# Gate matmuls between the up-phase tiles: groups of four quads at 24 tiles, in place of one or two quads at each of 77

## The reference, cut to what matters

```
s1, i1 = top_k(s[:, :, 0], 16);  s2, i2 = top_k(s[:, :, 1], 16)   # per head, 128 keys each
top, pos = top_k(s1 + s2 over 16x16, 16)                          # 8 heads x 16 = 128 routes a token
eidx  = (i1 * 128 + i2) at pos;  gates = softmax(top)
act   = gelu(x . u[eidx])
out   = sum over routes of (gates * act) * v[eidx]
```

## Time and profile before

| | |
|---|---|
| median of 3 runs | 3015.55 us (3014.22, 3015.55, 3023.57) |
| span of the profiled execution | 3015.1 us |
| TensorE matmul busy | 2968.4 us (98%) |
| VectorE busy | 2369.0 us (79%) |
| ScalarE busy | 1201.5 us (40%) |
| GpSimd busy | 1315.3 us (44%) |
| gate matmuls (L1702) | 1536, from 517.6 to 882.7 us in layer 0 and from 2068.8 to 2433.9 us in layer 1 |

### The profile page before, as it was taken

How to read it: one execution, slowest core, us unless ns; L and a number is a source line. 1 busy time by engine, 2 the same in 40 slices (tenths; PEclk the granted TensorE clock), 3 DMA queues, 4 the chain that set the end, 5 groups by cost and what they waited for, 6 DMA issues and landing times.

```text
span 3015.1 us, 43969 instructions
## 1 busy us (share of the span) xinstructions
PE 2968.4 (98%) x16132; PEld 2622.5 (87%) x16132; DVE 2369.0 (79%) x4437; ACT 1201.5 (40%) x1878; POOL 1315.3 (44%) x749
## 2 busy tenths in 40 slices
PE   8999999999999999999999999999999999999999
PEld 6668999999998888888888888999999997888887
DVE  7436899988886888888356737999888968888887
ACT  5434333444443333333435643334444433333333
POOL 4213465444434444443346533564434434544441
PEclk9999999999999999999999999999999999999999
DMA  4203367999999999999321122558999999999996
GB/s 147 69 29 105 105 203 263 341 370 361 375 368 368 381 362 354 366 356 338 105 98 43 35 84 85 172 175 319 364 371 362 375 360 374 363 354 377 360 362 223
DMA packets 345861, 800.83 MB, mean 266 GB/s; under 512 B 27952, under 2 KB 192048, under 8 KB 345392
## 3 DMA queue, kind: packets, MB, share of 16 engines
q1 hardware_dynamic: 271776, 529.49, 50.0%
q0 software_dynamic: 73728, 268.47, 23.6%
q10 hardware_dynamic: 144, 0.07, 0.0%
HBM read 695.15 MB, written 102.76 MB: 265 GB/s over the span
## 4 chain that ended last, share of the span: by engine, by line
PE 91%; DVE 3%; DMA 3%; ACT 1%; issue 1%; SPq 0%; POOL 0%; DVEq 0%; ACTq 0%
PE PS L1522 28%; PE PS L1524 27%; PE PS L1523 27%; PE PS L1702 3%; DMA arena<-acts_dram 1%; DMA gates_dram<-arena 1%; PE PS L1773 1%; PE PS L1679 1%; PE PS L1656 1%; DVE resid L1031 1%; PE PS L1639 1%; PE PS L1638 0%; ACT arena L654 0%; PE PS L1646 0%; POOL w_lo L567 0%
## 5 line engine op out<-in xcount | busy, mean ns | idle before, releaser
L1522 PE MATMUL PS<-x_hi,w_hi 128*128 128x384 f32 (+1 forms) x2616 | 927.0, 354 | 8.7 <-POOL w_lo L567 4.0
L1524 PE MATMUL PS<-x_hi,w_lo 128*128 128x384 f32 (+1 forms) x2616 | 907.4, 347 | 0.0
L641 ACT ACTIVATE w_hi<-w_raw 128x1024 fp32r<-128x1024 f32 x609 | 643.0, 1057 | 661.0 <-PE PS L1524 645.2
L1523 PE MATMUL PS<-x_lo,w_hi 128*128 128x384 f32 (+1 forms) x2616 | 905.6, 346 | 0.0
L578 POOL DMA_INDIRECT arena<-in_v_t,arena x256 | 443.0, 1731 | 566.4 <-DVE resid L1294 515.2
L1522 PE MATMUL PS<-w_hi,x_hi 128*128 128x512 f32 x1744 | 679.5, 390 | 7.6 <-DVE x_lo L1311 7.5
L1524 PE MATMUL PS<-w_hi,x_lo 128*128 128x512 f32 x1744 | 678.6, 389 | 0.0
L1523 PE MATMUL PS<-w_lo,x_hi 128*128 128x512 f32 x1744 | 678.5, 389 | 0.0
L567 POOL TENSOR_TENSOR w_lo<-w_raw,w_hi 128x1024 fp32r<-128x1024 f32 x169 | 420.5, 2492 | 549.4 <-ACT w_hi L641 549.3
L1271 DVE TENSOR_TENSOR w_lo<-w_raw,w_hi 128x1024 fp32r<-128x1024 f32 x440 | 536.9, 1220 | 110.5 <-ACT w_hi L641 110.3
L578 POOL DMA_INDIRECT arena<-in_u_rows,arena x256 | 382.6, 1495 | 485.6 <-DVE arena L1278 432.3
(11 more groups left out here) (186 smaller groups left out, 2358.2 us busy)
## 6 DMA issues: line engine op xcount, KB each, us to landing
w_raw<-in_u_t SPq DMA_DIRECT2D x256, 512.0 KB, 7.0
w_raw<-in_v_t SPq DMA_DIRECT2D x256, 512.0 KB, 5.7
acts_dram<-arena SPq DMA_DIRECT2D x256, 192.0 KB, 7.4
gates_dram<-arena SPq DMA_DIRECT2D x24, 2048.0 KB, 16.3
arena<-gates_dram SPq DMA_DIRECT2D x64, 768.0 KB, 7.7
arena<-acts_dram SPq DMA_DIRECT2D x256, 192.0 KB, 7.3
w_raw<-in_hg_t SPq DMA_DIRECT2D x40, 512.0 KB, 3.2
w_raw<-in_pq_t SPq DMA_DIRECT2D x32, 512.0 KB, 3.3
```

Source lines behind the costliest of these rows:

```text
L641: act.activation(w_hi[:, slot, :], w_raw[:, slot, :], ACT.Copy).then_inc(hi_ready, 1)
L1522: pe.matmul(ps, wh, xh, start=start, stop=False)
L1523: pe.matmul(ps, wh, xl, start=False, stop=False)
L1524: return pe.matmul(ps, wl, xh, start=False, stop=stop)
```

## The change

`quads_before` now rises in steps of four. A whole group of four quads (32 matmuls) is issued ahead of 24 of the tiles 44, 47, 50, 53, 57, ... 117 (19 distances of three tiles, four of four), in place of one quad at 58 and two quads at 19 of the 77 tiles from 41 to 117. ScalarE's moves and SyncE's stores go by the same function. The two octets of a group are built at VectorE's steps one and two after the group before it (`octets_at`), and at steps 41 and 42 for the first. The matmuls, their operands, the number of moves, stores and octets are the same.

```diff
+def steps_before(tile, count, first, end):
+    return count * min(max(tile - first, 0), end - first) // (end - first)
+
 def quads_before(tile):
-    return QUADS * min(max(tile - FIRST_QUAD, 0), END_QUAD - FIRST_QUAD) // (END_QUAD - FIRST_QUAD)
+    return 4 * steps_before(tile, QUADS // 4, FIRST_QUAD, END_QUAD)
+
+def group_at(group):
+    return next(tile for tile in range(NKEYS) if quads_before(tile + 1) > 4 * group)
+
+def octets_at(step):
+    first = [FIRST_QUAD] + [group_at(g) + 1 for g in range(QUADS // 4 - 1)]
+    return [2 * g + b for g, at in enumerate(first) for b in range(2) if step == at + b]
...
-                octet = 0
                 for s in range(FIRST_DVE_LOW - RING + 1, 2 * NKEYS):
...
-                    while octet < QUADS // 2 and 2 * octet < quads_before(s + 2):
+                    for octet in octets_at(s):
                         make_onehots(octet)
-                        octet += 1
```

## The result

In executions of both kernels on the same chip the changed kernel took 3025.51 us (median of 16 runs, 3018.05 to 3034.16), the kernel before 3018.0 us (median of 16, 3013.5 to 3023.86). The ratio is 1.0027, interval 1.0019 to 1.0035. Forecast were 3007.1 us and a range up to 3011.5. The forecast stood on 3015.55 us, the median of three runs of the kernel before; its sixteen give 3018.0, so 2.5 us of the distance between 3007.1 and 3025.51 are the starting point's.

What follows compares the result with a forecast made beforehand. TensorE, busy 98% of the span, was taken as the bound. Removing 106 visits at 0.080 us saves 8.5 us, all else nothing: 3015.1 - 8.5 = 3006.6, with the median 0.5 above, 3007.1 us; range 3004.8 to 3011.5.

Steps and rivals of the forecast that it cites:

- The unit costs: TensorE's gate matmuls: fixed 0.080 us per visit, 0.447 per quad, 1.87 per group; 106 visits removed save 8.5 us.
- Rival 3: TensorE's gate matmuls: a run of 32 goes slower past its 16th matmul; net +24 us, 3039 us; chance 0.04.
- Rival 4: TensorE's gate runs: the further matmuls gain 1.9 us by dense running, 3005.2 us; chance 0.03.
- ScalarE's moves cost nothing: ScalarE: four moves in a row end at V + 4.0 (V: group start), before Gelu is due at V + 6.0; no cost.
- VectorE's octets cost nothing: VectorE: same number of octets, moved by up to two steps, hidden behind three tiles of up matmuls; no cost.
- SyncE's queue: ... Not moved, no new wait: SyncE: gate stores are issued at multiples of eight quads, on the same tiles in both orders; no cost.
- It does not fall behind for good: VectorE: its work over three tiles with a group sums to 13.1 of 14.35 us, so it keeps up.
- The octets' slack: VectorE: a group's second octet ends 2.9 us before the next group is due; today's has 3.9 us.
- Rival 1: Ahead of gate matmuls TensorE waits for an octet delayed through Gelu's late stores; 4 us given back, 3011 us; chance 0.08.
- Rival 2: Start of the value phase: last gate store and loads behind it fixed in time, gain all lost, 3015.5 us; chance 0.05.

Runs made afterwards that it cites:

- experiment 11: The changed kernel with each gate store one SyncE step (one tile) earlier, still 2 MB on SyncE's queue: 3000.55 us, ratio 0.9946 to the kernel before.
- experiment 3: The changed kernel with ScalarE's four moves behind the Gelu and `w_hi` of their step instead of ahead: 3023.98 us, ratio 1.0022 to the kernel before.
- experiment 6: The changed kernel without the low f16 part of the second one-hot in VectorE's octets, TensorE reading the high part twice: 3027.19 us, ratio 1.0032.
- experiment 4: The changed kernel with groups of two quads, each with one octet, made two steps ahead as before: 3017.6 us, ratio 0.9996 to the kernel before.
- experiment 7: The changed kernel with only the last gate store of each layer on ScalarE's queue: 3025.92 us, ratio 1.0032 to the kernel before.
- experiment 1: The changed kernel with all gate stores issued from ScalarE's queue instead of SyncE's: 3005.8 us, ratio 0.9953 to the kernel before.
- experiment 5: The changed kernel with each gate store cut into four 512 KB parts on SyncE's queue: 3006.65 us, ratio 0.9963 to the kernel before.
- experiments 1 and 2: Gate stores on ScalarE's queue, in the changed kernel (3005.8 us, ratio 0.9953) and in the kernel before (3013.45 us, 0.9988).

## Why the prediction was wrong

- **The unit costs (0.080 us per visit, 0.447 per quad, 1.87 per group): right.** 1.86 us for 45 of 48 groups, and in experiment 11 the 8.46 us arrive whole.
- **Rival 3, a run past its 16th matmul goes slower: refuted.** 32 in a row go at the pace of 8. The figure of 81 ns that the Trainium skill gives ("TensorE: Matmul & The Clock Gate", section "Back-to-back issue gap") doesn't hold in these runs either: the trace shows 55.3 to 55.8 ns. Rival 4, denser running, didn't come either.
- **ScalarE's moves cost nothing: right,** by experiment 3. VectorE's octets cost nothing by their load, as far as experiment 6 can show it; by their place they do, as the next two points say.
- **"SyncE's queue: ... Not moved, no new wait": this is the step that failed.** The tile of the gate store is unchanged, as I wrote. But a step of SyncE waits for a `w_lo`, and the gate store now goes out between two `w_lo` with no octet between them, behind the group's second octet: 3.2 us later against TensorE's tiles, and 1.6 us ahead of the next load, not 4.2. Gelu's room fell from 7.7 to 4.8 us by it. I counted the position in the order and not the time. Nor did I look at what stands behind the gate store: its 21.06 us in the chain and Gelu's longest wait for a store, 4.5 us, were both read, and not connected. The timeline of SyncE in the kernel before shows the hold (593.59, 4.83 us) and would have priced it.
- **"It does not fall behind for good": wrong for the loop.** VectorE's own sum, 13.1 of 14.35 us, is right, but the loop of store, Gelu, `w_hi`, `w_lo` and SyncE has no such slack. The octets' slack was worked out as 2.9 us from one undisturbed place; by the starts in the trace its least is 0.1 us where TensorE doesn't wait, and 2.7 before (behind the first two octets of a layer). In experiment 11, where the loop is left in peace, it is 3.6 us and more at all but one of them (1.8).
- **Rival 1 was the right mechanism with the wrong size.** I took Gelu's five late stores as fixed in number and in length (1.8 us), and counted coincidences. They aren't fixed: the change makes them 22, up to 8.9 us. Three groups wait, which is fewer than the five a layer that I priced, but one alone cost 4.0 us, since the clock fell behind it. The term was priced by a longest wait of 1.8 us in the kernel before; nothing in those rows says what the change would make of it.
- **Rival 2's counter-argument was wrong.** I wrote that the last gate store follows `w_lo` of tile 122, "which follows TensorE's own tiles", and so comes earlier. With the lag it comes 12.0 us behind the start of tile 118, not 7.9: at 898.0 us, 3 us later, though TensorE is 1.0 us earlier. SyncE waits for its landing before it loads the first gates, so the value phase starts later by as much. The loss there (7.4 us) is larger than that in the gate stretches (5.0).
- **The size of the miss is in part the starting point's:** 2.5 us, as said above. The range would have been missed without them too.

**What stays open.** How the nearer deadline divides between the second octet ahead of `w_lo` and the uneven pace of the tiles (5.94 us with a group, 4.2 without): experiments 4 and 11 point to the first, but none holds the other fixed. How fast the lag runs off was not measured. More than four buffers for Gelu results was not tried. Why a gate store takes 29 us to land in experiment 7 and 16 in experiment 11 was not looked into. Nor was the stretching of single value tiles (in the trace of experiment 1 tiles 3 and 5 of layer 1 take 5.14 and 5.78 us, in that of 11 4.08 and 4.39). No execution of the changed kernel near its median was profiled, so for 4.5 us of the loss there is only the mean clock to go by.

## What to carry to other kernels

When work is regrouped, look at each queue that issues "at the same step" as before and ask what that step waits for: if the wait moves by a few microseconds, everything behind it in the queue moves too. A long transfer in an in-order queue has a room that can be read beforehand (the end of the issues behind it against the first deadline), and where it is near zero a gain on the bounding engine turns into a loss. Then place the transfer just ahead of a natural pause of its queue: one step earlier turned +0.27% into -0.54% here. In the traces 5.0 us of that came in the gate stretches and 16.7 at the start of the value phase, where the last of these transfers lands earlier. Where a program waits for the landing of all of them before its next phase, read that landing against the phase's start too.

## What the runs showed of the hardware

- The issue behind a store of 2 MB in 512-byte pieces is held on the same queue, a load or a store alike. It ended 9.6 to 17.4 us behind the start of the gate store with the change and 8.3 to 14.5 before; in experiment 11, where it was due later, 7.7 to 13.1. A load due within 2 us took 9.98, 10.84, 14.39 and 16.01 us, a store 11.82. Behind 0.5 MB the issue took 0.8 us in the median and 7.0 at most (experiment 5). With the store on ScalarE's queue, SyncE's next issue took 0.33 us each of 48 times (experiments 1 and 2). The Trainium skill ("DMA: Bandwidth & Descriptors", section "Rules for kernel authors") says that spreading transfers over engines doesn't help bandwidth and "only saves sequencer issue time". Experiments 1 and 2 agree: the gate stores land no sooner (24.1 us, 16.1 with the change). What the other queue, together with the earlier issue, was worth: 0.12% in one order, and in the other the step from 1.0027 to 0.9953.
- TensorE idle for 2.24 us, and for 4.4 and 4.7, was followed each time by a stretch at a granted 0.50 (775.6 to 778.6, 932.3 to 935.7, and 2485.8 to 2488.5 with matmuls 0.43 us apart, not 0.23). A wait of 1.8 us (layer 1, 2476.7) was not. The length of the wait doesn't decide it alone: 2.0 us in experiment 4 (2479.4) was followed by one, 2.6 us in the kernel before (2498.4 to 2501.0) was not. The price of the first rose from 2.24 to 4.00 us by it. It may also be why the changed kernel's runs spread over 16 us and those of experiment 11 over 5; the mean granted clock of the runs fits that (0.992 to 0.997, and 0.996 to 0.998), but it was not tested.
- 32 matmuls of 128 columns in f16 in a row go at 55 ns, as 8 do.
